# Products of a hybrid decoder layer over 258 instead of 260 query columns, with the row buffers moved by 56 bytes

## What is computed

```python
h = concatenate([meta, x])                      # 272 rows
xn = rmsnorm(h); proj = xn @ w_in               # 2048 x N_IN
ya = fox_attention(qa, ka, va, logf) @ w_a_o    # branch A
yb = (sc_b * causal_dwconv3(sc_c * sc_h)) @ w_b_o   # branch B
yc = (silu(rc) * rmsnorm(gla(qc, kc, vc, g))) @ w_c_o   # branch C
mix = sum(sigmoid(gate_i) * y_i)                # gates are columns of proj
h = h + mix @ w_o
u = causal_dwconv3(rmsnorm(h) @ w_up)           # 2048 x 11264
h = h + (silu(u_gate) * u_up) @ w_down          # 5632 x 2048
return rmsnorm(h)[16:]                          # 256 rows leave
```

## Time and profile before

| | |
|---|---|
| median of 3 runs | 1738.51 us (1738.46 to 1738.52) |
| the profiled execution, its time | 1738.35 us |
| its span, first to last instruction | 1736.5 us |
| outside the span | 1.85 us |
| TensorE matmuls busy | 1725.9 us, 99% of the span |
| VectorE, ScalarE, GpSimd busy | 1117.6, 763.9, 263.5 us |
| DMA | 185 GB/s in the mean |

### The profile page before, as it was taken

How to read it: one execution, slowest core, us unless ns; L and a number is a source line. 1 busy time by engine, 2 the same in 40 slices (tenths; PEclk the granted TensorE clock), 3 DMA queues, 4 the chain that set the end, 5 groups by cost and what they waited for, 6 DMA issues and landing times.

```text
span 1736.5 us, 34095 instructions
## 1 busy us (share of the span) xinstructions
PE 1725.9 (99%) x13429; PEld 1674.7 (96%) x13429; DVE 1117.6 (64%) x1607; ACT 763.9 (44%) x921; POOL 263.5 (15%) x494
## 2 busy tenths in 40 slices
PE   9999999999999999999999999999999999999998
PEld 8999999999999999999999999999999999888886
DVE  6857766667565555555556687777777777644554
ACT  6635454354354443444444444334444434343443
POOL 4153332630530000000000033421000000000000
PEclk9999999999999999999999999999999999999999
DMA  8667657666566665566655566666555655656664
GB/s 234 170 180 187 169 149 199 176 177 177 153 188 182 184 177 184 171 192 193 195 168 191 184 192 197 205 200 189 184 181 181 189 183 175 229 192 191 191 194 134
DMA packets 310299, 320.67 MB, mean 185 GB/s; under 512 B 17353, under 2 KB 285133, under 8 KB 310093
## 3 DMA queue, kind: packets, MB, share of 16 engines
q1 hardware_dynamic: 296861, 311.01, 59.6%
q0 software_dynamic: 12928, 7.80, 2.0%
q10 hardware_dynamic: 432, 0.79, 0.1%
HBM read 311.10 MB, written 2.11 MB: 180 GB/s over the span
## 4 chain that ended last, share of the span: by engine, by line
PE 98%; DVE 1%; DMA 0%; ACT 0%; issue 0%; SPq 0%; ACTq 0%; DVEq 0%
PE ps L1438 81%; PE ps L1717 5%; PE ps L1715 5%; PE ps L1716 5%; PE ps L1545 1%; DVE xl L942 0%; PE ps L1559 0%; DMA xa<-in_meta_tokens_dram 0%; PE ps L1584 0%; PE ps L1574 0%; DVE lo L897 0%; PE ps L1575 0%; PE ps L1603 0%; PE ps L1604 0%; PE ps L1531 0%; PE ps L1520 0%
## 5 line engine op out<-in xcount | busy, mean ns | idle before, releaser
L897 DVE TENSOR_TENSOR lo<-raw,hi 128x1024 fp32r<-128x1024 f32 x584 | 710.0, 1229 | 485.0 <-ACT hi L628 482.7
L628 ACT CAST hi<-raw 128x1024 fp32r<-128x1024 f32 x584 | 605.3, 1049 | 663.6 <-PE ps L1438 535.5
L1438 PE MATMUL ps<-xh,hi 128*128 128x260 f32 (+1 forms) x3312 | 532.9, 283 | 0.2 <-DVE xl L942 0.2
L1438 PE MATMUL ps<-xl,hi 128*128 128x260 f32 (+1 forms) x3312 | 530.0, 282 | 0.0
L1438 PE MATMUL ps<-xh,lo 128*128 128x260 f32 (+1 forms) x3312 | 529.6, 282 | 0.0
L1438 PEld LDWEIGHTS ps<-xh,hi 128*128 128x128 f32 x3312 | 452.4, 188 | 1.4 <-issue 0.4
L1438 PEld LDWEIGHTS ps<-xl,hi 128*128 128x128 f32 x3312 | 452.2, 188 | 0.0
L1438 PEld LDWEIGHTS ps<-xh,lo 128*128 128x128 f32 x3312 | 452.1, 188 | 0.0
L611 POOL DMA_DIRECT2D hT<-h2b x128 | 69.3, 550 | 602.1 <-DVE h2b L1290 597.3
L1717 PE MATMUL ps<-lo,act_h 128*128 128x512 f32 x350 | 137.3, 392 | 0.0
L1716 PE MATMUL ps<-hi,act_l 128*128 128x512 f32 x350 | 136.8, 391 | 0.0
(11 more groups left out here) (304 smaller groups left out, 1251.4 us busy)
## 6 DMA issues: line engine op xcount, KB each, us to landing
raw<-in_w_in_dram SPq DMA_DIRECT2D x224, 512.0 KB, 3.8
raw<-in_w_up_dram SPq DMA_DIRECT2D x176, 512.0 KB, 4.6
raw<-in_w_down_dram SPq DMA_DIRECT2D x88, 512.0 KB, 4.7
raw<-in_w_o_dram SPq DMA_DIRECT2D x32, 512.0 KB, 3.7
raw<-in_w_in_dram SPq DMA_DIRECT2D x32, 256.0 KB, 4.1
raw<-in_w_a_o_dram SPq DMA_DIRECT2D x16, 512.0 KB, 4.5
raw<-in_w_b_o_dram SPq DMA_DIRECT2D x16, 512.0 KB, 3.8
raw<-in_w_c_o_dram SPq DMA_DIRECT2D x16, 512.0 KB, 3.4
```

The costliest lines, as they stand in the source:

```text
L628: nc.scalar.copy(part(ph, i, q, hi_all), raw[:, s, :]).then_inc(hi_ready, 1)
L897: nc.vector.tensor_tensor(part(ph, i, q, lo_all), raw[:, s, :], part(ph, i, q, hi_all).bitcast(F32), ALU.subtract).then_inc(lo_ready, 1)
L1438: ins = nc.tensor.matmul(pset(st, n)[:, m, a:], tiles(weights, s, j, m), moving(j)[side][:, a:], start=first and (kind, at) == (0, 0), sto ...
```

## The change

Nothing changes its place in any engine's order. Three things differ. Products over the query columns, in all of GT, WO, UP and in groups 2, 7 and 8 of BR, take 258 columns from token 14 instead of 260 from token 12. They write PSUM columns 2 to 259, where their readers look. The buffers `xh, xl`, `bo_h, bo_l` and `mix_h, mix_l` begin 14 elements (56 bytes) later within an allocation that is 64 bytes longer.

A window from token 14 (56 bytes on) now begins at 91168 + 56 + 56 = 91280, again 16 past a multiple of 64. The windows that keep their columns begin elsewhere: those over 272 columns at 24 past a multiple of 64 (32 before), those over 260 columns (groups 0 and 1, the first half of group 3) at 8 past one (16 before). `act_h` and `act_l` stay where they were, since `AH` is smaller by the 16 elements that `xn_rows` has gained.

```diff
+        STEP = 14
         xn_scope = ExitStack()
-        xh = sb("xh", [P, KT, T], F32R, xn_scope)
-        xl = sb("xl", [P, KT, T], F32R, xn_scope)
+        xn_rows = sb("xn_rows", [P, 16 + 2 * KT * T], F32R, xn_scope)
+        xh = xn_rows[:, STEP:STEP + KT * T].rearrange("p (k t) -> p k t", t=T)
+        xl = xn_rows[:, STEP + KT * T:STEP + 2 * KT * T].rearrange("p (k t) -> p k t", t=T)
...
-        bo_h = sb("bo_h", [P, 3, BKT, T], F32R, br_out)
-        bo_l = sb("bo_l", [P, 3, BKT, T], F32R, br_out)
+        bo_rows = sb("bo_rows", [P, 16 + 2 * 3 * BKT * T], F32R, br_out)
...
-        mix_h = sb("mix_h", [P, KT, T], F32R, gtt)
-        mix_l = sb("mix_l", [P, KT, T], F32R, gtt)
+        mix_rows = sb("mix_rows", [P, 16 + 2 * KT * T], F32R, gtt)
...
-        AH, AL = 48, 32
+        AH, AL = 32, 32
...
-                            ins = nc.tensor.matmul(pset(st, n)[:, m, a:], tiles(weights, s, j, m), moving(j)[side][:, a:],
+                            acc = pset(st, NC)[:, m, QW:] if n == NQ else pset(st, n)[:, m, a:]
+                            ins = nc.tensor.matmul(acc, tiles(weights, s, j, m), moving(j)[side][:, a:],
...
-            window = [(C0, NC)] * 3 + [(0, T)] * 4 + [(C0, NC)] * 2
+            window = [(C0, NC)] * 2 + [(Q0, NQ)] + [(0, T)] * 4 + [(Q0, NQ)] * 2
...
-                        mv = x_window(kq * KJ, C0, NC)
+                        mv = x_window(kq * KJ, Q0, NQ)
...
-                    use_turns(WO, i, q, st, (lambda k0: lambda j: (mix_h[:, k0 + j, C0:T], mix_l[:, k0 + j, C0:T]))(kq * KJ),
-                              NC, kq == 0, kq == 3)
+                    use_turns(WO, i, q, st, (lambda k0: lambda j: (mix_h[:, k0 + j, Q0:T], mix_l[:, k0 + j, Q0:T]))(kq * KJ),
+                              NQ, kq == 0, kq == 3)
...
-                    use_turns(UP, i, q, st, x_window(kq * KJ, C0, NC), NC, kq == 0, kq == 3)
+                    use_turns(UP, i, q, st, x_window(kq * KJ, Q0, NQ), NQ, kq == 0, kq == 3)
```

More of the change, by code:

```diff
@@ L221, in hybrid_layer @@
         br_out = ExitStack()
-        bo_h = sb("bo_h", [P, 3, BKT, T], F32R, br_out)
-        bo_l = sb("bo_l", [P, 3, BKT, T], F32R, br_out)
+        bo_rows = sb("bo_rows", [P, 16 + 2 * 3 * BKT * T], F32R, br_out)
+        bo_h = bo_rows[:, STEP:STEP + 3 * BKT * T].rearrange("p (g k t) -> p g k t", t=T, g=3)
+        bo_l = bo_rows[:, STEP + 3 * BKT * T:STEP + 2 * 3 * BKT * T].rearrange("p (g k t) -> p g k t", t=T, g=3)
         brt = ExitStack()
@@ L287, in hybrid_layer @@
         gtt = ExitStack()
-        mix_h = sb("mix_h", [P, KT, T], F32R, gtt)
-        mix_l = sb("mix_l", [P, KT, T], F32R, gtt)
+        mix_rows = sb("mix_rows", [P, 16 + 2 * KT * T], F32R, gtt)
+        mix_h = mix_rows[:, STEP:STEP + KT * T].rearrange("p (k t) -> p k t", t=T)
+        mix_l = mix_rows[:, STEP + KT * T:STEP + 2 * KT * T].rearrange("p (k t) -> p k t", t=T)
         gate = sb("gate", [P, 3, 2, NQ], F32, gtt)
@@ L1663, in gate_trip @@
                         st, before = (g + 1) % 2, 1 + (g + 1) // 2
-                        mv = (lambda g, k0: lambda j: (bo_h[:, g, k0 + j, C0:T], bo_l[:, g, k0 + j, C0:T]))(g, kq * KJ)
+                        mv = (lambda g, k0: lambda j: (bo_h[:, g, k0 + j, Q0:T], bo_l[:, g, k0 + j, Q0:T]))(g, kq * KJ)
                         last = 1
@@ L1670, in gate_trip @@
                         pe.wait_ge(pads_zero, 6)
-                    use_turns(GT, i, q, st, mv, NC, kq == 0, kq == last, turned(q // 4 + 1) if q < 12 and not settled else ROWS)
+                    use_turns(GT, i, q, st, mv, NQ, kq == 0, kq == last, turned(q // 4 + 1) if q < 12 and not settled else ROWS)
                     if first and q < SCQ:
```

## The result

The changed kernel takes 1757.78 us in the median of four runs (1757.17 to 1757.87), the kernel before 1738.49 us; the ratio is 1.0111, 95% interval 1.0096 to 1.0126. The forecast was 1732.8 us and a range up to 1743.

A forecast was written before the change was run, and what follows sets the result against it. TensorE's steps were taken to bound the kernel: 1738.35 - 8.0 (columns) + 2.3 (new beginnings) = 1732.65 us, put at 1732.8 us for the median, with a range from 1726 to 1743 us.

The forecast's parts named there:

- What bounds the kernel: TensorE's matmuls fill 99% of the span; with the count fixed, only the distance between two starts can change.
- Both signs: Set to prove the prediction wrong: trains over 258 columns at 118.3 ns or more, or 272s costing 2 ns more.
- The columns: 9,600 matmuls in GT, WO, UP and part of BR go from 260 to 258 columns: 0.83 ns each, 8.0 us less.
- my three prices for two columns: 0.83 ns by the clock, 0.98 by the 260- and 272-column trains, 0.86 by DN's 256 and 512 columns.
- the two rows that did speak of the place: Line 1603, 2 ns more for a row beginning off 16 bytes; DN, 4.2 ns between two beginnings of moving tiles.
- The new beginnings: 2,304 matmuls over 272 or 260 columns now begin 8 bytes past a multiple of 16: 1 ns each, 2.3 us more.
- my bound of 4.2 ns: Upper price of a new beginning, from DN's 512-column matmuls at two kinds of beginning; 9.7 us over 2,304 matmuls.
- What costs nothing: PSUM columns, VectorE and ScalarE row addresses, DMA queues and prologue writes of xl: put at 0, prologue below 1 us.
- The pace that the train falls into: Rival: 258-column trains run at the unsettled pace less two columns, 119.2 ns a step, 1748.8 us; 13 in 100.
- The train settles better: Rival: stalls fall and a step drops by 1.67 ns, 16.0 us gained, 1724.8 us; 7 in 100.
- The rule of lines of 16 bytes: SBUF is read in 16-byte lines; 258 and 260 columns both touch 65, making the columns' term 0 instead of 8.0 us.
- The formula of the gap: Matmul gap of N / 2.4 plus some 2.5 ns: supports 0.83 ns for two columns, gives 110.8 ns for 260.

The follow-up runs named there:

- the fourth experiment: The changed kernel with hi and lo 64 bytes further on and every other TensorE operand where it was modulo 256: 1770.55 us.
- the kernel with an order for each phase: The changed kernel with block orders 1, 0, 2, 3 on xh and xl, 0, 3, 1, 2 on branch rows, 3, 2, 0, 1 on the mixture: 1748.03 us.

## Why the prediction was wrong

**What bounds the kernel** was read rightly: TensorE's steps, and their sum gives the whole result. Both signs that the prediction set for being wrong came: trains over 258 columns at 118.3 ns or more, and the 272s 4.0 ns dearer.

**The columns**, the step "I take 0.83 ns", failed. It rested on the sentence that these products go on beginning 16 bytes past a multiple of 64, as if that fixed the step. It does not: it depends on the distance to the weight tiles modulo 256 as well. The runs gave these steps in ns, each the mean of a train or of all trains on a pair of buffers, for the order of places that 0, 3, 1, 2 makes:

| place against the weights | 0 | 64 | 128 | 192 |
|---|---|---|---|---|
| 260 columns | 118.3 | 120.8 | 119.8 | 119.2 |
| 258 columns | 121.5 to 121.7 | 120.0 to 120.2 | 116.7 or 121.7 | 120.4 |

Before, all three pairs stood at 0, the best column for 260 and no good one for 258. The move of 56 bytes kept the byte modulo 64 and put xh and xl at 64: 120.0 in place of the forecast 117.5. The term was 8.0 us less and measured 11.5 us more (11.9 + 1.6 - 2.0). Only the branch rows, at 128 because the allocation of xh and xl ahead of them had grown by 64 bytes, gained, 1.7 ns a matmul, twice what I gave them.

Of my three prices for two columns (0.83 to 0.98 ns) one was the clock's and two were slopes between other widths, 260 to 272 and 256 to 512. They agreed, but none compared two widths of these products at one place, and the two rows that did speak of the place, I used for the kept windows alone.

**The new beginnings**, the term of 2.3 us, was mis-sized: 7.7 us (2.36 + 5.37). The price was 2.8 ns for 260 and 4.0 for 272 columns and not 1. It was within my bound of 4.2 ns, but not for my reason. Rows moved 64 bytes, with no byte off 16, already cost the 272s 2.3 ns, and 258 columns that begin 8 past a multiple of 16 ran at 119.2 ns, better than at three of the four places. The price of an odd beginning by itself was not isolated.

**What costs nothing** held: no new waits on line 1443, VectorE and ScalarE within 2.1 us as busy as before, and with the 8 bytes in PSUM taken away the time was 1757.51 against 1757.78 us.

**The rivals.** The pace that the train falls into was named, with 13 in 100, and put at 119.2 ns by taking two columns off the 120.0 ns of the earlier trace rows. It was 120.0, so 1748.8 us was short by 9: 3.5 us in the products over 258 columns, and 5.4 in the kept windows. "The train settles better" got 7 in 100 and exists as well, 116.7 ns, at place 128. That both existed should have widened the range; it ended at 1743 with one of them at 1749 and no reason against it but that the settled pace comes back in every phase. In the kernel before all buffers stood at one place, so this said nothing of another place. Nor did the pace come back everywhere. The prediction took 120.0 ns for a pace before a train settles; in GT's first trip all 144 matmuls on the branch rows kept it, 17.27 us, although later trips have 118.3 ns at the same addresses and order:

```profile
520.15 0.64 PE L1438 MATMUL ps<-bo_h,hi 128*128 128x260 f32 x4
...
537.42 0.64 PE L1438 MATMUL ps<-xh,hi 128*128 128x260 f32 x4
```

So the trace of before already held a train with two paces.

**The rule of lines of 16 bytes** in the Trainium skill's "SBUF — State Buffer" would make 258 and 260 columns equal, 65 lines each. The runs show neither equality nor a clock's worth: by the table 258 columns are 3.2 to 3.4 ns dearer at place 0, 0.6 to 0.8 cheaper at 64, 3.1 cheaper or 1.9 dearer at 128, 1.2 dearer at 192.

**The formula of the gap** in the Trainium skill's "TensorE: Matmul & The Clock Gate", section "Back-to-back issue gap", is given there for an isolated matmul and makes 110.0 ns of 258 columns. No long train over 258 columns here came below 116.6, and the formula has no term for places; the measurement decides.

**What stays open.** Why the step depends on a distance modulo 256 is not shown; that reads of rows and of weights get in each other's way is an argument that fits the fourth experiment and no more. That a train has two paces at one place and order is shown: 116.7 and 121.7 ns for the branch rows in the change and in the kernel with an order for each phase, and for UP on the two sides of line 1706. What in an entry decides is not: some breaks of the order switch the pace and others don't, and a single other product does too. So each value of the table may be one of two or three; at place 0 these were 120.0 and 121.7 ns for 258 columns and 118.3 and 120.0 for 260. Other distances between rows than 64 modulo 256 and other distances between weight tiles were not tried.

## What to carry to other kernels

When TensorE is full and steps cost more than their columns, compare the same product on different buffers and in different phases of one trace: a difference at equal width comes from addresses, the order, or what ran ahead, and it can outweigh the columns that are saved. When a buffer moves or a window shifts, hold the distance between moving and stationary operand modulo 256, or sweep it: of four places, 260 columns were fastest at 0 and 258 at 128. Where a cyclic order of products runs at a good pace, try the same turn of the order in the next phase; it was worth 18.2 us here.

## What the runs showed of the hardware

With fp32r operands, the mean step of a 258-column matmul in a train varied from 116.6 to 121.7 ns at the granted clock of 2.4 GHz, by addresses, the order of blocks and what ran before. Moving the weights by 64 bytes had the same effect as moving the rows the other way, to 0.2 ns: 121.6 against 121.5 ns at distance 0, 120.2 against 120.0 at 64, 116.7 against 116.7 at 128. The same products at the same addresses in the same order took 466.7 or 486.7 ns for each four matmuls, by what ran before them; a train held either pace for a thousand matmuls or more, and changed it within a panel behind some turns of the order and behind one product of another form.
